# Scores of the first two heads inside the values' projection, in two attentions of a two-block transformer kernel, and a new order of the last attention's projections

## The reference

```python
# first block, dilated attention ("a"): 8 heads of 64
q, k, v = split(rms_norm(x, norm_mix_g) @ w_in)          # 512 columns each
q, k = rms_norm(to_heads(q), qnorm_a_g), rms_norm(to_heads(k), knorm_a_g)
o = softmax(q @ k.T / 8 + bias) @ v

# second block, last attention ("m")
k, v = split(rms_norm(h, kv_norm) @ w_kv_shared, 2)      # 256 columns each, 4 heads
k = rms_norm(to_heads(k), k_norm_shared)
q = rms_norm(to_heads(rms_norm(h, ln_mix[1]) @ b_w_q), b_q_norm)   # 1024 columns, 16 heads
o = softmax(q @ k.T / 8 - slope * distance) @ v           # causal
h = h + o @ b_w_out
```

## Time and profile before

| | |
|---|---|
| median of 3 runs | 1077.8 us (1074.75 to 1078.85) |
| the profiled execution | 1077.36 us, its span 1075.6 us |
| PE busy | 1022.8 us, 95% of the span |
| DVE busy | 766.0 us, 71% |
| ACT busy | 701.2 us, 65% |
| granted TensorE clock, mean | 0.99 |
| first scores of `att_a` / of `att_m` | 95.1 us / 789.2 us after the span's start |

### The profile page before, as it was taken

How to read it: one execution, slowest core, us unless ns; L and a number is a source line. 1 busy time by engine, 2 the same in 40 slices (tenths; PEclk the granted TensorE clock), 3 DMA queues, 4 the chain that set the end, 5 groups by cost and what they waited for, 6 DMA issues and landing times.

```text
span 1075.6 us, 17447 instructions
## 1 busy us (share of the span) xinstructions
PE 1022.8 (95%) x6136; PEld 853.4 (79%) x6136; DVE 766.0 (71%) x1347; ACT 701.2 (65%) x1201; POOL 96.8 (9%) x181
## 2 busy tenths in 40 slices
PE   7988899999998999899999999999989999999998
PEld 6876789999997877787788778767878688877866
DVE  5686557666666657778668878877777668888876
ACT  6665545444445536575588989857676489899855
POOL 9017000000000100000420000000000330000000
PEclk9999999999999999999999999999999899999999
DMA  9871027666654555004439999854424429999951
GB/s 295 288 254 40 1 96 237 186 185 181 188 176 166 160 189 198 1 2 157 176 131 317 350 335 332 302 192 148 128 78 157 176 88 319 339 337 338 329 169 40
DMA packets 106156, 209.25 MB, mean 195 GB/s; under 512 B 7736, under 2 KB 51744, under 8 KB 105824
## 3 DMA queue, kind: packets, MB, share of 16 engines
q1 hardware_dynamic: 103584, 204.04, 55.7%
q0 software_dynamic: 2064, 3.25, 1.1%
q10 hardware_dynamic: 432, 0.99, 0.2%
HBM read 207.19 MB, written 1.06 MB: 194 GB/s over the span
## 4 chain that ended last, share of the span: by engine, by line
PE 85%; DVE 7%; ACT 4%; issue 2%; DMA 1%; ACTq 0%; SPq 0%; POOL 0%; DVEq 0%; POOLq 0%
PE bank L882 23%; PE bank L1639 17%; PE bank L1658 11%; PE bank L1312 8%; PE bank L1322 8%; PE bank L997 4%; PE bank L986 2%; PE bank L976 2%; PE bank L786 2%; PE bank L2139 1%; PE bank L1680 1%; PE bank L1469 1%; PE bank L1507 1%; PE bank L1650 1%; DMA expert_w<-in_moe_w_up 1%
## 5 line engine op out<-in xcount | busy, mean ns | idle before, releaser
L882 PE MATMUL bank<-weight_parts,x_high 128*128 128x512 f32 (+2 forms) x768 | 223.2, 375 | 8.6 <-ACT x_high L850 2.6
L1639 PE MATMUL bank<-expert_high,block_high 128*128 128x256 f32 x560 | 183.8, 328 | 3.4 <-ACT block_low L1587 2.4
L1567 DVE TENSOR_TENSOR expert_low<-expert_w,expert_high 128x1024 fp32r<-128x1024 f32 x140 | 164.7, 1219 | 9.9 <-ACT expert_high L1560 9.5
L882 PEld LDWEIGHTS bank<-weight_parts,x_high 128*128 128x128 f32 x768 | 139.1, 188 | 35.6 <-ACT x_high L850 7.0
L1639 PE MATMUL bank<-expert_high,block_low 128*128 128x256 f32 x560 | 158.2, 282 | 0.0
L1639 PE MATMUL bank<-expert_low,block_high 128*128 128x256 f32 x560 | 158.0, 282 | 0.0
L903 DVE TENSOR_TENSOR weight_parts<-ring,weight_parts 128x1024 fp32r<-128x1024 f32 (+3 forms) x112 | 121.1, 1104 | 51.2 <-ACT weight_parts L900 50.7
L900 ACT CAST weight_parts<-ring 128x1024 fp32r<-128x1024 f32 (+3 forms) x112 | 104.4, 958 | 75.6 <-PE bank L882 55.4
L1560 ACT CAST expert_high<-expert_w 128x1024 fp32r<-128x1024 f32 x140 | 140.2, 1053 | 19.3 <-DMA expert_w<-in_moe_w_up 18.9
L882 PE MATMUL bank<-weight_parts,x_low 128*128 128x512 f32 (+2 forms) x384 | 143.1, 373 | 0.0
L1658 PE MATMUL bank<-expert_w,junk 128*128 128x512 f32 x280 | 131.3, 592 | 0.0
(11 more groups left out here) (356 smaller groups left out, 1693.2 us busy)
## 6 DMA issues: line engine op xcount, KB each, us to landing
expert_w<-in_moe_w_gate SPq DMA_DIRECT2D x70, 512.0 KB, 5.7
expert_w<-in_moe_w_up SPq DMA_DIRECT2D x70, 512.0 KB, 7.4
expert_w<-in_moe_w_down SPq DMA_DIRECT2D x70, 512.0 KB, 5.5
ring<-in_w_ff SPq DMA_DIRECT2D x64, 512.0 KB, 3.9
ring<-in_w_in SPq DMA_DIRECT2D x16, 512.0 KB, 8.5
ring<-in_a_w_in SPq DMA_DIRECT2D x16, 512.0 KB, 6.6
ring<-in_ple_w_gate SPq DMA_DIRECT2D x16, 512.0 KB, 5.7
ring<-in_w_o SPq DMA_DIRECT2D x8, 512.0 KB, 4.4
```

What stands on the lines that cost most here:

```text
L882: mm = nc.tensor.matmul(bank[:, j["m"] % 4, 0:n], j["operand"][x][:, 2 * c + kk, at[0]:at[1]], weight_parts[:, number % PAIRS, w, kk * n:( ...
L1567: nc.vector.tensor_tensor(half_of(expert_low[:, b % DEPTH, 0:2048], j), half_of(expert_w[:, b % DEPTH, 0:2048], j), half_of(expert_high[:, ...
L1639: mm = nc.tensor.matmul(bank[:, 4 + b % 2, 0:256].rearrange("p (q n) -> p q n", q=2), x[:, b % 2, k, :], w[:, k], start=k == 0 and n == 0, ...
```

## The change

Four edits.

1. **Values' projection of `att_a`.** PE does the scores of heads 0 and 1 ahead of the fourth chunk of `l_va` (`first_pair_of_a`); `pe_attention` begins with heads 2 and 3 alone. DVE does the biases of these two heads before it takes its bank of `l_va`, and the two `dve_root` of the other attention are moved, one ahead of the transposed heads, one behind the two biases. ACT waits for the last matmul of `l_va` before the first exponential.
2. **`att_n`** gets the same split of its first four scores, but with nothing between the pairs.
3. **Projections of `att_m`.** The order is first query half `l_mq0` (with `t_kv` ahead of its third chunk), keys `l_k`, second query half `l_mq1`, values `l_v`. SP loads the weights in that order. The norm of each part follows on ACT and DVE in the same order.
4. **Start of `att_m`.** Inside `l_v` PE transposes the keys ahead of chunk 1, the first query half ahead of chunk 2, and does the scores of heads 0 and 1 ahead of chunk 3. The second query half is transposed inside the attention, behind the first head's turned probabilities and ahead of the first values (`turn_last_heads`). Arithmetic and number of instructions are otherwise the same.

```diff
-    l_q = linear(a["b_w_q_2"][0], KB, D_MODEL, x_parts, moba_q, "copy", n_moba)
     t_kv = turn(h, KB, [(kv_high, gains["kv_norm"], kv_low)])
+    l_mq0 = linear(a["b_w_q_2"][0], KB, 512, x_parts, moba_q, "copy", n_moba, at=0)
     l_k = linear(a["w_kv_shared_2"], KB, 256, (kv_high, kv_low), moba_kv, "copy", n_moba, at=0)
+    l_mq1 = linear(a["b_w_q_2"][0], KB, 512, x_parts, moba_q, "copy", n_moba, at=512)
     l_v = linear(a["w_kv_shared_2"], KB, 256, (kv_high, kv_low), moba_kv, "copy", n_moba, at=256)
-    run(l_q + l_k + l_v)
+    run(l_mq0 + l_k + l_mq1 + l_v)
...
-    def pe_linear(pe, jobs, turned_by=(), turn_ahead=None):
+    def pe_linear(pe, jobs, turned_by=(), ahead=None):
...
-                if turn_ahead is not None and group[0] is jobs[0] and c == 2:
-                    pe_turn(pe, turn_ahead)
+                if ahead is not None and group[0] is jobs[0] and c in ahead:
+                    ahead[c]()
...
-        scores_of_four(first, here[0:4])
+        scores_of_pair(pe, first + 2, here[2:4])
...
             if j + 1 < len(here):
                 turn_probs(first + j + 1)
...
+            if j == 0 and before_values is not None:
+                before_values()
             values(first + j, here[j])
...
@@ tensor
-        pe_linear(pe, l_va, turn_ahead=t_a)
-        wait_turned(pe, t_a)
+        def first_pair_of_a():
+            wait_turned(pe, t_a)
+            wait_took(pe, l_ukv)
+            scores_of_pair(pe, att_a["first"], att_a["heads"][0:2])
+
+        pe_linear(pe, l_va, ahead={2: lambda: pe_turn(pe, t_a), 3: first_pair_of_a})
         wait_took(pe, l_va)
         pe_attention(pe, att_a, by_four=True)
...
-        pe_linear(pe, l_q[0:2], t_moba)
-        pe_turn(pe, t_kv)
-        pe_linear(pe, l_q[2:4])
+        pe_linear(pe, l_mq0, t_moba, ahead={2: lambda: pe_turn(pe, t_kv)})
         pe_linear(pe, l_k, t_kv)
-        pe.wait_ge(dve_scaled, 4)
-        pe_linear(pe, l_v, turn_ahead=t_mq[0])
-        pe.wait_ge(dve_scaled, 5)
-        pe_turn(pe, t_mq[1])
-        pe.wait_ge(pool_scaled, 5)
-        pe_turn(pe, t_mk)
-        wait_turned(pe, t_mk + t_mq[0] + t_mq[1])
...
+        pe_linear(pe, l_mq1)
+        pe_linear(pe, l_v, ahead={1: turn_keys_of_m, 2: turn_first_heads, 3: first_pair_of_m})
         wait_took(pe, l_v)
-        pe_attention(pe, att_m, by_four=True)
+        pe_attention(pe, att_m, by_four=True, before_values=turn_last_heads)
@@ scalar, last attention
+        take_turn(act, t_kv, "act")
+        take_linear(act, l_mq0, "act")
+        wait_took(act, l_mq0)
+        for t in range(TILES):
+            squares(rows[:, 0, t * 512:(t + 1) * 512], moba_q[:, t, 0:512], last=t == 1)
+        act.wait_ge(sums_ready, 7)
+        act_root(act, r_mq0)
         take_linear(act, l_k, "act")
...
+        take_linear(act, l_mq1, "act")
...
+        take_turn(act, t_mk + t_mq0, "act")
         act.wait_ge(sums_ready, 9)
-        act_root(act, r_mk)
+        act_root(act, r_mq1)
         nc.scalar.preload_act_table(ACT.Exp)
-        take_turn(act, t_mq[0], "act")
+        exps_of(act, att_m["first"])
         take_linear(act, l_v, "act")
-        take_turn(act, t_mq[1], "act")
-        take_turn(act, t_mk, "act")
-        act_attention(act, att_m, by_four=True)
+        exps_of(act, att_m["first"] + 1)
+        take_turn(act, t_mq1, "act")
+        act_attention(act, att_m, by_four=True, begun=2)
@@ vector, dilated attention
+        dve_root(dve, r_bq, scale_ready)
         take_turn(dve, t_a, "dve")
         dve_latent_sums(dve)
+        dve.wait_ge(toep_ready, 32)
+        for i in range(2):
+            bias_head(dve, att_a["first"] + i, att_a["heads"][i])
+        dve_root(dve, r_bk, scale_ready)
         take_linear(dve, l_va, "dve")
-        dve_root(dve, r_bq, scale_ready)
-        dve_root(dve, r_bk, scale_ready)
-        dve.wait_ge(toep_ready, 32)
-        dve_attention(dve, att_a, by_four=True)
+        dve_attention(dve, att_a, by_four=True, begun=2)
```

More of the change, by code:

```diff
@@ L957, in probT_of, with scores_of_pair, scores_of_four, pe_attention @@
         return (act_probT, dve_probT)[n % 2], n // 2 + 1
-    def pe_attention(pe, s, compressed=False, by_four=False):
+    def scores_of_pair(pe, n, pair):
+        for lo, hi, keys in ((0, P, P), (P, 2 * P, 2 * P)):
+            for i, x in enumerate(pair):
+                rows_here = slice(64 * i, 64 * i + 64)
+                at = 0 if lo == 0 else P
+                mm = nc.tensor.matmul(bank[:, (n + i) % 4, at:at + keys], x["q"][rows_here, lo:hi],
+                                      x["k"][rows_here, 0:keys], start=True, stop=True)
+                if lo:
+                    mm.then_inc(scores_made, 1)
+    def scores_of_four(pe, n, four):
+        if n >= 4:
+            pe.wait_ge(biased, n)
+        scores_of_pair(pe, n, four[0:2])
+        scores_of_pair(pe, n + 2, four[2:4])
+    def pe_attention(pe, s, compressed=False, by_four=False, before_values=None):
         def scores(n, x):
@@ L966, in scores @@
                              stop=True).then_inc(scores_made, 1)
-        def scores_of_four(n, four):
-            if n >= 4:
-                pe.wait_ge(biased, n)
-            for pair in (0, 2):
-                for lo, hi, keys in ((0, P, P), (P, 2 * P, 2 * P)):
-                    for i, x in enumerate(four[pair:pair + 2]):
-                        rows_here = slice(64 * i, 64 * i + 64)
-                        at = 0 if lo == 0 else P
-                        mm = nc.tensor.matmul(bank[:, (n + pair + i) % 4, at:at + keys], x["q"][rows_here, lo:hi],
-                                              x["k"][rows_here, 0:keys], start=True, stop=True)
-                        if lo:
-                            mm.then_inc(scores_made, 1)
         def turn_probs(n):
@@ L1016, in pe_attention @@
             if j % 4 == 0 and j + 4 < len(here):
-                scores_of_four(first + j + 4, here[j + 4:j + 8])
+                scores_of_four(pe, first + j + 4, here[j + 4:j + 8])
             if j + 1 < len(here):
@@ L1057, in act_attention @@
         for j in range(count + 1):
-            if j < count:
-                exps(first + j)
+            if begun <= j < count:
+                exps_of(act, first + j)
             if by_four and j and j % 2 == 0:
@@ L1119, in dve_attention @@
                     mix_core(first // 4 + j // 4 - 2, s["cores"][j // 4 - 2])
-                if j < len(here):
-                    bias(first + j, here[j])
+                if begun <= j < len(here):
+                    bias_head(dve, first + j, here[j])
                 if at == 0 and j:
@@ L2184, in _ @@
         pe.wait_ge(own_ready, 2)
+        scores_of_pair(pe, att_n["first"], att_n["heads"][0:2])
         pe_attention(pe, att_n, compressed=True, by_four=True)
@@ L2586, in _ @@
         dve_root(dve, r_mk, scale_ready)
-        take_turn(dve, t_mq[0], "dve")
-        take_linear(dve, l_v, "dve")
-        take_turn(dve, t_mq[1], "dve")
-        take_turn(dve, t_mk, "dve")
-        dve_attention(dve, att_m, by_four=True)
+        take_linear(dve, l_mq1, "dve")
+        take_turn(dve, t_mk, "dve")
+        dve.wait_ge(squared, 9)
+        v.tensor_reduce(r_mq1["sum"], rows[:, 1, :].rearrange("p (h d) -> p h d", d=64), AX.X,
+                        ALU.add).then_inc(sums_ready, 1)
+        take_turn(dve, t_mq0, "dve")
+        dve_root(dve, r_mq1, scale_ready)
+        for i in range(2):
+            bias_head(dve, att_m["first"] + i, att_m["heads"][i])
+        dve.wait_ge(scale_ready, 8)
+        steepen(r_mq1, 8, 8)
+        take_linear(dve, l_v, "dve")
+        scale_heads(v, mq[:, :, 8:16, :], scales(r_mq1, 0, 8), dve_scaled)
+        for i in range(2, 4):
+            bias_head(dve, att_m["first"] + i, att_m["heads"][i])
+        take_turn(dve, t_mq1, "dve")
+        dve_attention(dve, att_m, by_four=True, begun=4)
         split_first(dve, l_moba_o, "dve", 0, 1)
```

135 lines of the change are left out of this document (72 added, 63 removed).

## The result

The change makes the kernel a little slower. The forecast was 1077.4 us, within 1071.5 to 1080.7.

What follows compares the result with a forecast made beforehand. The prediction took PE's idle time to bound the kernel. From the profiled 1077.36 us, -4.5 at att_a, 0 at att_n, +2.8 at att_m's start and +1.7 for its clock gave 1077.4 us, range 1071.5 to 1080.7.

Steps and rivals of the forecast that it cites:

- What bounds it: Whole kernel: PE's chain ends last, so a change pays by what it takes out of PE's idle time.
- `att_a`, -4.5 us: Start of att_a: next four scores 2.9 us sooner, and 1.6 us because the clock stays high.
- The bound: Start of att_a: -4.7 to -1.7 us, as one moved DVE step beside POOL may cost 1.2 us.
- `att_a`'s clock, 1.6 us of that: Start of att_a: PE idle about 1 us twice, clock stays high, 3.51 us to the first values becomes 1.90.
- the change does nothing at `att_a`: Rival at att_a: DVE's take is late beside POOL, gain 2.3 us less, 1079.7 us; chance 0.08.
- `att_n`, 0: At att_n: same eight matmuls in the same order and a wait already met, so no effect.
- `att_m`, the idle time of 3.3 us: Projections of att_m: PE newly idle 3.3 us ahead of the second query half, waiting for norm and split.
- `att_m`, its start, +2.8 us: Start of att_m: the new stall is just paid back, then ACT's copy delays the first values by 2.8 us.
- `att_m`'s clock, +1.7 us: At att_m: the clock falls after the 3.3 us idle time, 3.4 us at half rate lose 1.7 us.
- The sum: Whole kernel: 1077.36 - 4.5 + 2.8 + 1.7 = 1077.4 us.
- The slower rival: Clock falls twice at att_m and stays low at att_a: 1079.1 to 1080.7 us; chance 0.12, with its tail.

Runs made afterwards that it cites:

- a_late_root: DVE's steps for the keys' norm put behind the take and four biases, otherwise a_only; 1072.79 us, ratio 0.9976 to before.
- a_only: The kernel before with the edit at att_a alone (plus the att_n edit); 1077.38 us against 1076.63, ratio 1.0004.
- the first runs: First measurement of the whole change against the kernel before, 11 runs each; median 1082.19 us against 1074.8, ratio 1.0056.
- the second: The whole change measured once more beside other kernels, 12 runs; median 1080.57 us against 1075.39 before, ratio 1.0045.
- m_only: The kernel before with the att_m edits alone (plus the att_n edit); 1084.05 us, ratio 1.0069; measured again 1081.19 us, ratio 1.0057.
- m_fill: m_only with 14 extra matmuls, result overwritten, in PE's idle time ahead of the second query half; 1077.15 us, ratio 1.0008 to before.
- after_fill: The whole change plus 14 extra matmuls in PE's idle time ahead of the second query half; 1081.22 us, ratio 1.0042 to before.
- late_stall: The whole change with DVE's keys' norm steps behind the take and four biases at att_a, idle time at att_m kept; 1078.51 us, ratio 1.003 to before.
- late_fill: late_stall with 14 extra matmuls in PE's idle time at att_m; 1078.43 us, ratio 1.0008 to before.
- m_gap: m_only with two early splits of the second query half, plus an added PE wait ahead of that half; 1079.92 us, ratio 1.0033 to before.
- m_fill7: m_only with 7 extra matmuls in PE's idle time ahead of the second query half; 1079.48 us, ratio 1.0021 to before.

## Why the prediction was wrong

- **What bounds it.** Right: PE's idle time was what counted.
- **`att_a`, -4.5 us: the step that failed.** "The first two biases and the norm steps are by then done: they fit into the 2.59 us that DVE waited ahead of the take and the 0.8 us added." They don't. DVE is busy without a break from 87.4 to 99.1 us. Two of the steps lie beside POOL's two instructions, and each waits for the end of one: 2.0 us more than 2 x 0.17. A step of the other norm, 1.08 us beside POOL, comes on top. The bound allowed for one such step; that POOL's row is two instructions (x2), and so two stops, was in the earlier trace rows of my own reading. The next four scores start 13.21 us behind `t_a` (101.46 - 88.25), before 14.18 (100.93 - 86.75): 1.0 us gained instead of 2.9. In `a_late_root` it is 11.56 (99.94 - 88.38): 2.6.
- **`att_a`'s clock, 1.6 us of that.** It rested on idle times near 1 us. They were 2.58 and 0.75, and from the next four scores to the first values it was 3.56 us (105.02 - 101.46), before 3.51; in `a_late_root` 1.90, to the hundredth the figure that the forecast took from `att_m`. The products behind them are slow for longer (1.48 us against 0.83), which takes the 1.0 us gained as well. `a_only` shows the same over its runs: 2.0 us gained, 2.2 lost by the clock. So the term is 0, not -4.5. That is the rival "the change does nothing at `att_a`", given 0.08: its mechanism was right, its price of 2.3 us half of the true one, since it left out the clock.
- **`att_n`, 0.** Right in the trace: from its first scores to its first values 5.31 us (438.62 - 433.31), before 5.32 (438.52 - 433.20). No run takes this edit by itself.
- **`att_m`, the idle time of 3.3 us.** Right: 3.25. The chain runs as it was laid out, through the same lines.
- **`att_m`, its start, +2.8 us.** Right in size: 3.1, with the wait for ACT's copy 1.78 us. But the reading of it, that the idle time was paid back and the copy's wait was the loss, holds only as a sum. Taking the idle time away gave 3.4 us of place, halving the copy's wait 0.9.
- **`att_m`'s clock, +1.7 us.** Right for this fall: 5 of 6 executions fell, for 3.4 us each, 1.7 us. The profiled one of the changed kernel did not; that it lies 1.7 us below the median isn't explained by it, since its mean clock (0.988) is that of the eleven runs. Part of the argument was luck: it took 1.67 us as an idle time that doesn't lower the clock, and in `a_late_root` the clock fell behind just that one.
- **The sum.** 1077.36 + 0 + 3.1 + 1.7 = 1082.2 us, the median of the first runs; 1080.57 was that of the second. That the first agrees to the tenth is luck: the 1077.36 us of the profiled execution are 2.6 above the median of the before beside it (1074.8). By the ratios the change costs 6.0 and 4.8 us, the terms give 4.8. What was wrong, 4.5 us, stands in one term.
- **The slower rival** (the clock low at `att_a` and at `att_m`) had the other half of what happened, at 1080.7. By the Trainium skill, "TensorE: Matmul & The Clock Gate", section "Part 4: PE-mode transpose", transposes don't count as activity for the clock gate as other matmuls do; with the eight transposes at the new start of `att_m` and its short idle times the clock fell there in 4 of 14 profiled executions, and at the old start, behind twelve transposes, in 1 of 3. So the traces bear out that it can fall, not that it does as a rule, and no run tells the transposes from the idle times.

Still open: why filling the idle time gave 5 to 7 us with the `att_m` edits alone and nothing with the whole change. The clock's cost over the runs (`m_only` 14.6 and 11.9, `m_fill` 8.0; after 12.7 and 12.6, `after_fill` 11.6; `late_stall` 11.3, `late_fill` 10.2) always went down, by 1 us or by 4 to 7. In the profiles of `m_fill` and `after_fill` there is no fall at the second query half, and one at the attention's start. Both profiles of `m_only` have that second fall too, those of the changed kernel don't. Whether the filling brings it was not tried.

## What to carry to other kernels

Work that is moved ahead of a wait has to fit into that wait at the speed it has *there*: read which neighbour runs in that stretch, and how many instructions its row merges, before a step of 0.17 us is counted as one. When work is reordered so that a projection follows its predecessor sooner, look for what prepares its operands; two splits ahead of a norm were worth more than the whole reordering. And an idle time on TensorE is priced with what follows it: here 3.3 us of place and 1.7 us of slower matmuls.

## What the runs showed of the hardware

- A DVE step on 128x16 values, of one tensor operand (L748, 1.19 us) or two (L747, 1.15 us), waits for the end of a POOL instruction on two operands; both take 0.17 us without one. DVE's biases beside POOL, which read the matmuls' memory, keep their 0.29 and 0.42 us (100.20 to 101.32, POOL's L952 beside them). The Trainium skill, "SBUF — State Buffer", section "SBUF: two separate sides", says that DVE instructions with two inputs in SBUF or in a mode with two ports share a pair of ports with GpSimd as an exclusive lock, held for the whole instruction; the ends that coincide (88.77 with 88.74, 97.04 with 96.97, 98.26 with 98.23) agree with it. In which mode L748 and L745 run, with one tensor operand, no run shows.
- The clock falls where PE starts again behind 3.2 us of idle time, not within it: in `m_gap` the window in which PE does nothing has the granted clock 1.00, the two after it 0.65 and 0.50. So the dense matmuls that follow pay.
- Shorter idle times can be followed by a fall too, where only transposes, scores and products with values surround them: a fall followed the 2.49 us at 445 us in 11 of the 17 profiled executions, and the 1.67 us at the old start of `att_m` in 1 of 3. None followed the 1.64 us between dense matmuls in the one execution of `m_fill7`.
- The clock of one kernel falls in one execution and not in the next: behind the 3.25 us it fell in one of the two profiled executions of the changed kernel. The stretch at 445 us, the same in all kernels, had scores of 2.47 us before, of 2.93 after, of 1.58 in `a_only`. One profile doesn't settle what an idle time costs; 12 runs of each kernel left an uncertainty of some 1.7 us either way.
